# Odd layer of a two-layer decoder step: rotation, turning and convolution beside the input projection, GpSimd's cosine products one chunk behind VectorE's sine products

## The chip, the cores and the metric

The kernel runs on one core of a Trainium2 chip. A core has five engines, each with an instruction stream of its own: TensorE (PE in the rows), VectorE (DVE), ScalarE (ACT), GpSimd (POOL) and SyncE (SP, which here only issues DMAs). They meet only through semaphores and barriers. The metric is device time in microseconds (us) of one launch. Differences of 0.2% (about 4 us) or more can be told from no change.

## What is computed

One inference step of two layers for 528 prompt positions (16 learned ones and 512) and 32 sample positions (8 sequences of 4). The two sets lie side by side as 560 columns all through the kernel. The changed part belongs to layer 1, the odd one:

```
rq, rk, rv, rg, lx, lgate = split(xn @ w_in_odd, 6 parts of 512 columns)
q = rotary(heads(rq), pos);  k = rotary(heads(rk), pos) * 128**-0.5;  v = heads(rv)
rotary(x): concat([x1*cos - x2*sin, x1*sin + x2*cos])        # x1, x2: halves of a head of 128
retention per head and chunk: S_t = gamma*S_{t-1} + k_t^T v_t,  o_t = q_t S_t
hr = silu(rg) * layernorm_per_head(o)
u  = concat([conv_state, lx]);  xc = conv_b + sum_j conv_w[j] * u[:, j:j+T]      # 4 taps
r, ig = sigmoid of two block-diagonal products with xc
hs = linear recurrence (a from r; input from ig, xc and a);  hl = hs * gelu(lgate)
out = concat([hr, hl]) @ w_out_odd
```

RMSNorms stand before and behind it, and a gated feed-forward part follows. Layer 0 has its own mixer and the same kind of feed-forward part.

## The kernel before

**Layout.** Activations are held turned: 128 features on the partitions, 560 positions along the free axis. A "chunk" is one such 128 x 560 block. `proj` (`Pt`, named `projected` in the rows) has room for 28; the odd input projection fills 24: rq 0 to 3, rk 4 to 7, rv 8 to 11, rg 12 to 15, lx 16 to 19, lgate 20 to 23.

**Projection.** Each product is made of three: weights and inputs are split into a high and a low part, and high*high, high*low and low*high are added up. One output chunk is 8 contraction blocks x 3 products x 2 halves of 280 columns, 48 matmuls (L1919). ScalarE makes the high part of a weight piece (`in_high`, L2093), VectorE the low one (`low`, L2272) and copies the finished chunk from PSUM with the row scale (`in_evac`, L2431). There are two weight pieces (`w_h`, `w_l`) and four PSUM tiles of two banks each. SyncE fills a ring of two slots, each with one unit of 256 weight columns (two chunks). The first four chunks are made together with the norm in `first_tiles`; the other twenty in a hardware loop of five turns with four chunks each. All of that lies in `close_layer(0, ...)`, the block that ends layer 0, since the odd projection is joined to the last feed-forward product of layer 0.

**Between the blocks** stands a barrier of all engines. Three blocks follow the projection:

- Rotation. TensorE multiplies each of the eight q and k chunks by a 128 x 128 matrix `swap`, which exchanges the halves with a sign (L2536). VectorE multiplies the result by the sine (L2557), GpSimd the chunk itself by the cosine (L2547), VectorE adds (L2563). ScalarE scales k first (L2526). SyncE loads the rotation table, the retention state (8 DMAs of 256 KB, L2510), the decay table, the convolution state and the gate weights.
- Turning (`transposes`, L486). k and v are brought to position-major order: 12 jobs of 4 transposes; 5 small ones bring the samples' convolution and recurrence state over. VectorE and ScalarE copy the results in turns (L494, L500).
- Retention (`decayed_attention`). TensorE first runs 4 matmuls on constants (`warm`, L465), then 32 score tiles (L981). VectorE multiplies each by its decay (L1084), TensorE multiplies by v (L1004). For the samples' tile of each head it also multiplies by the loaded state (L1014, 8 small products). Behind every second score tile VectorE makes one of 16 steps of the convolution (`convolution`: L2619 and L2620 for the first tap, L2623 and L2625 for the other three).

State update, gates, recurrence, normalisation and layer 1's output projection come behind.

## Time and profile before

| | us |
|---|---|
| three runs, median (lowest, highest) | 1869.51 (1868.13, 1869.68) |
| the profiled run's own time | 1871.89 |
| its span, first to last instruction | 1870.3 |
| TensorE busy | 1683.5 (90% of the span) |
| VectorE / ScalarE / GpSimd busy | 835.4 / 458.2 / 297.3 |
| mean granted TensorE clock, full speed is 1 | 0.928 |

The rows below give times from the start of the span. A timeline row has its start, its length, the engine, the line in the code, the operation and the names written and read; in brackets stands how long the engine was idle before it and what released it. A row of stretches gives each engine's busy time in the stretch with the number of instructions that begin there, then the granted clock (1.00 is 2.4 GHz, 0.50 is 1.2 GHz), the share of the DMA engines and GB/s. Matmuls overlap in the pipeline, so that a matmul of 0.29 us can start every 0.13 us.

### The profile page before, as it was taken

Reading aid. Unit: us, or ns where it says so; the run is one execution under the profiler, and the core shown is the slowest. Engines: PE = TensorE matmul, PEld = TensorE weight load, DVE = VectorE, ACT = ScalarE, POOL = GpSimd, SP = SyncE. Lnnn points to the kernel's source line nnn. Section 1 sums busy time; section 2 is a strip of 40 time slices with the busy share of each in tenths; the row PEclk is TensorE's granted clock in tenths of the full one; section 3 lists DMA queues with packets and bytes.
Section 4 is the critical chain, followed back from the end, with each engine's and each line's share of the span. In section 5 each row is a group of like instructions: output and inputs, shape, how many; then the busy total and the mean of one; then the engine's idle time right before and its main releaser. Section 6 shows DMA issues by size and latency. Waiting matters only on the chain. (4 is left out here: it accounts for less than half of the span.)

```text
span 1870.3 us, 31120 instructions
## 1 busy us (share of the span) xinstructions
PE 1683.5 (90%) x12351; PEld 1539.9 (82%) x12351; DVE 835.4 (45%) x1551; ACT 458.2 (24%) x684; POOL 297.3 (16%) x368
## 2 busy tenths in 40 slices
PE   5999998698876999999999899979579999999996
PEld 4999954465645999999999889957378999999996
DVE  4332544544434664434322463356757544433225
ACT  4111311122212431222212321132334221222211
POOL 1411001001000033333200200030210333332000
PEclk9999987678997999999999899988779999999998
DMA  4322210132975122333333212230131232333321
GB/s 131 94 69 79 68 50 1 51 128 78 285 238 152 46 66 73 86 90 90 93 93 85 68 46 90 88 89 1 51 92 46 68 90 77 80 90 103 83 62 49
DMA packets 225254, 159.80 MB, mean 85 GB/s; under 512 B 18041, under 2 KB 206437, under 8 KB 225048
## 3 DMA queue, kind: packets, MB, share of 16 engines
q1 hardware_dynamic: 220832, 156.40, 28.7%
q0 software_dynamic: 3280, 1.85, 0.4%
q8 instruction: 49, 0.80, 0.2%
q10 hardware_dynamic: 1064, 0.51, 0.1%
q14 instruction: 29, 0.24, 0.0%
HBM read 149.11 MB, written 9.88 MB: 85 GB/s over the span
## 5 line engine op out<-in xcount | busy, mean ns | idle before, releaser
L2093 ACT CAST w_high<-ring 128x1024 fp32r<-128x1024 f32 (+1 forms) x148 | 165.4, 1118 | 749.4 <-PE psum L1919 718.5
L1919 PE MATMUL psum<-mixed_high,w_high 128*128 128x280 f32 x1472 | 310.6, 292 | 20.5 <-DVE mixed_low L2280 18.6
L1919 PE MATMUL psum<-mixed_high,w_low 128*128 128x280 f32 x1472 | 312.2, 293 | 0.0
L1919 PE MATMUL psum<-mixed_low,w_high 128*128 128x280 f32 x1472 | 309.5, 292 | 0.0
L2272 DVE TENSOR_TENSOR w_low<-ring,w_high 128x1024 fp32r<-128x1024 f32 (+1 forms) x148 | 237.3, 1603 | 138.3 <-ACT w_high L2093 136.2
L1919 PEld LDWEIGHTS psum<-mixed_high,w_high 128*128 128x128 f32 x1472 | 235.8, 190 | 21.7 <-DVE w_low L2272 19.4
L1919 PEld LDWEIGHTS psum<-mixed_high,w_low 128*128 128x128 f32 x1472 | 236.3, 190 | 0.0
L1919 PEld LDWEIGHTS psum<-mixed_low,w_high 128*128 128x128 f32 x1472 | 233.8, 189 | 0.0
L2453 POOL TENSOR_TENSOR silu<-silu,rstd 128x560 f32<-128x560 f32 x44 | 61.4, 1394 | 551.7 <-DVE silu L2352 551.7
L2352 DVE TENSOR_TENSOR silu<-silu,psum 128x280 f32<-128x280 f32 x88 | 35.3, 443 | 155.9 <-PE psum L1919 154.3
L348 PE MATMUL psum<-normed_high,w_high 128*128 128x280 f32 x448 | 94.3, 292 | 0.6 <-PEq L531 0.6
L348 PE MATMUL psum<-normed_high,w_low 128*128 128x280 f32 x448 | 93.8, 290 | 0.0
L348 PE MATMUL psum<-normed_low,w_high 128*128 128x280 f32 x448 | 93.5, 290 | 0.0
L1919 PE MATMUL psum<-hidden_low_b,w_high 128*128 128x280 f32 x308 | 90.0, 292 | 0.0
L1919 PE MATMUL psum<-hidden_high_b,w_high 128*128 128x280 f32 x308 | 90.0, 292 | 0.0
L1919 PE MATMUL psum<-hidden_high_a,w_high 128*128 128x280 f32 x308 | 89.8, 292 | 0.0
L1919 PE MATMUL psum<-hidden_high_b,w_low 128*128 128x280 f32 x308 | 89.6, 291 | 0.0
L1919 PE MATMUL psum<-hidden_high_a,w_low 128*128 128x280 f32 x308 | 89.6, 291 | 0.0
L1919 PE MATMUL psum<-hidden_low_a,w_high 128*128 128x280 f32 x308 | 89.5, 291 | 0.0
L1919 PE MATMUL psum<-normed_b,w_high 128*128 128x280 f32 x320 | 88.0, 292 | 0.0
L2352 DVE TENSOR_TENSOR silu<-rstd,psum 128x280 f32<-128x280 f32 x88 | 35.3, 442 | 110.5 <-PE psum L1919 110.3
L348 PEld LDWEIGHTS psum<-normed_high,w_high 128*128 128x128 f32 x448 | 71.1, 188 | 1.1 <-issue 1.1
(460 smaller groups left out, 3289.7 us busy)
## 6 DMA issues: line engine op xcount, KB each, us to landing
ring<-in_ffn_wd SPq DMA_DIRECT2D x16, 1408.0 KB, 7.0
ring<-in_ffn_wg SPq DMA_DIRECT2D x40, 512.0 KB, 4.0
ring<-in_ffn_wu SPq DMA_DIRECT2D x40, 512.0 KB, 5.2
projected<-in_cache_fox_k SPq DMA_DIRECT2D x64, 256.0 KB, 4.3
ring<-in_w_in_even SPq DMA_DIRECT2D x14, 1024.0 KB, 5.3
ring<-in_w_in_odd SPq DMA_DIRECT2D x12, 1024.0 KB, 5.1
v_pages<-in_cache_fox_v SPq DMA_DIRECT2D x32, 256.0 KB, 3.7
projected<-in_cache_fox_v SPq DMA_DIRECT2D x16, 256.0 KB, 3.2
```

What stands on the lines that cost most here:

```text
L348: last = nc.tensor.matmul(banks[2 * tl + half][:, 0:HALF], w[:, k, :], m[:, half * HALF:(half + 1) * HALF], start=(kk == 0 and w is w_high ...
L1919: done = mm(banks[2 * tl + a][:, 0:HALF], w, m[a], start=first and s == 0, stop=last and s == 2)
L2093: nc.scalar.copy(dst, src).then_inc(w_hi[p], 1)
L2272: v.tensor_tensor(dst, src, high_.bitcast(F32), ALU.subtract).then_inc(w_lo[p], 1)
L2352: last = v.tensor_tensor(silu[:, slot, c], silu[:, slot, c] if p else rstd[:, c], banks[2 * q + a][:, 0:HALF], ALU.mult)
L2453: g.tensor_tensor(silu[:, slot, :], silu[:, slot, :], rstd[:, :], ALU.mult)
```

## The change

The rotation block and the turning block go. Their work, and the convolution, is put among the last twenty chunks of the projection, whose loops are written out on every engine:

- The order of the units becomes q, k, lx, v, rg, lgate (`UNITS`). From the ninth chunk on only two PSUM tiles are used in place of four, so that banks 4 to 7 are free for turning.
- Rotation without the matrix: VectorE multiplies each half of a chunk by the sine and writes it to the other half's partitions of a scratch tile (two 64 x 560 products, the sign is in the table). GpSimd multiplies the chunk by the cosine. VectorE adds one chunk later. The scaling of k is four ScalarE instructions.
- The convolution is four VectorE steps, one tap for all four chunks each, behind the chunks n = 14 to 17 in order.
- TensorE turns behind n = 10 and 11 (the small jobs) and behind n = 15 to 20 (two jobs of four transposes each); ScalarE copies all of them.
- Rotation table, convolution state, recurrence state, gate weights and decay tables are loaded during the projection. The retention state is loaded in the retention block, and TensorE waits for it at the first head's samples.
- Memory is laid out anew: the mixer's output lies in `proj`, and the gates' and the recurrence's buffers are tiles of their own. The constant `swap` and its load go.

```diff
             def _(sp):
...
+                    send(sp, units[1], slot, UNITS[slot])
+                    sp.dma_start(decays[slot], io["c_decay"][:, slot, :]).then_inc(decay_in, 16)
...
+                sp.wait_ge(used[1], DOWN_END + 2)
+                sp.dma_start(rope, io["c_rope"]).then_inc(rope_full, 16)
+                sp.dma_start(conv_in, io["state_lru_conv"].rearrange("b j n -> (b j) n")).then_inc(lru_in, 16)
+                sp.dma_start(h0_in[:, :], io["state_lru_h"].rearrange("b (k p) -> (b k) p", p=128)).then_inc(lru_in, 16)
+                for s in range(4, 12):
+                    when_split(29 + s)
+                    send(sp, units[1], s % 2, UNITS[s])
+                    if s == 5:
+                        sp.wait_ge(lru_zero, 1)
...
             def _(pe):
-                with pe.Fori(1, 6) as i:
-                    for q in range(4):
...
+                for n in range(4, 24):
+                    p, t = n % 2, in_tile(n)
+                    pe.wait_ge(w_lo[p], 31 + n // 2)
+                    pe.wait_ge(tile_evac[t], (15, 11, 14, 11)[t] + (1 if n < 8 else 2 + (n - 8) // 2))
...
+                    if n == 15:
+                        pe.wait_ge(rotated, 8)
...
+                    for j in TURNS_AT.get(n, ()):
+                        turn(j)
...
             def _(act):
+                for n in range(4, 24):
+                    if n + 2 < 24:
+                        in_high(n // 4, n % 4)
+                    if 6 <= n < 10:
+                        c = n - 6
+                        act.wait_ge(tile_evac[c], (15, 11, 14, 11)[c] + 2)
+                        nc.scalar.mul(Pt[:, 4 + c, :], Pt[:, 4 + c, :], QK_SCALE).then_inc(rk_scaled, 1)
+                    for j in TURNS_AT.get(n, ()):
+                        act.wait_ge(turned, j + 1)
...
             def _(dve):
+                def rotate(i):
+                    x, tmp = Pt[:, i, :], rtmp[i % 2]
...
+                    v.drain()
+                    v.tensor_tensor(tmp[0:64, :], x[64:128, :], rope[64:128, 1, :], ALU.mult)
+                    v.tensor_tensor(tmp[64:128, :], x[0:64, :], rope[0:64, 1, :], ALU.mult).then_inc(rot_sin, 1)
+                def add_rotated(i):
+                    dve.wait_ge(rot_cos, i + 1)
+                    v.tensor_tensor(Pt[:, i, :], Pt[:, i, :], rtmp[i % 2][:, :], ALU.add).then_inc(rotated, 1)
...
+                for n in range(24):
+                    in_evac(n)
+                    if n == 0:
+                        in_low(0, 1, 33)
+                    if 4 <= n < 22:
+                        in_low((n // 2 + 1) % 2, n % 2, 32 + n // 2)
+                    if 5 <= n < 13:
+                        rotate(n - 5)
+                    if 6 <= n < 14:
+                        add_rotated(n - 6)
...
+                    if 14 <= n < 18:
+                        convolve(n - 14)
             def _(pool):
+                    for i in range(2 * MH):
+                        pool.wait_ge(rot_sin, i + 1)
+                        g.tensor_tensor(Pt[:, i, :], Pt[:, i, :], rope[:, 0, :], ALU.mult).then_inc(rot_cos, 1)
...
 def decayed_attention(...)
+                    if state_in is not None and hd == 0:
+                        pe.wait_ge(state_in, 16 * 8)
```

The names in the rows of the two orders are those of the program; `token_major` holds the products with the sine before the change, `rotated` after it. On TensorE, from the last matmuls of the projection to the first score of the retention, stands before the change:

```order
L1919 MATMUL psum<-normed_b_6575,w_low_6554 128x280
L2079 REGISTER_ALU
L2079 COMPARE_AND_BRANCH
L1860 UNCONDITIONAL_BRANCH
L2528 UNCONDITIONAL_BRANCH
L2536 MATMUL psum<-projected,swap 128x280 x16
L2505 UNCONDITIONAL_BRANCH
L479 UNCONDITIONAL_BRANCH
L486 MATMUL psum<-ident,projected 128x128 x16
L486 MATMUL psum<-ident,projected 16x128 x4
```

The multiplications by `swap` leave the program. The transposes move up to places within the projection. On TensorE behind the chunk n = 15 stands now:

```order
L1961 MATMUL psum<-normed_b_6579,w_high_6557 128x280
L1961 MATMUL psum<-normed_high_a_6577,w_low_6558 128x280
L1961 MATMUL psum<-normed_b_6579,w_low_6558 128x280
L2132 MATMUL psum<-ident,projected 128x128 x8
L1961 MATMUL psum<-normed_high_a_6577,w_high_6557 128x280
L1961 MATMUL psum<-normed_b_6579,w_high_6557 128x280
```

Eight transposes stand there, and the next chunk's 48 matmuls behind them; n = 16 to 20 have the same. On VectorE the rotation block has this piece eight times before the change (two of them shown, behind the block's entry):

```order
L2431 TENSOR_TENSOR projected<-psum,rstd 128x280 x4
L1860 UNCONDITIONAL_BRANCH
L2549 UNCONDITIONAL_BRANCH
L2557 TENSOR_TENSOR token_major<-psum,projected 128x280 x2
L2563 TENSOR_TENSOR projected<-projected,token_major 128x560
L2557 TENSOR_TENSOR token_major<-psum,projected 128x280 x2
L2563 TENSOR_TENSOR projected<-projected,token_major 128x560
```

After the change a chunk's turn on VectorE in the projection (here n = 6 and the start of n = 7) reads:

```order
L2508 TENSOR_TENSOR projected<-psum,rstd 128x280 x2
L2349 TENSOR_TENSOR w_low_6558<-ring,w_high_6557 128x1024
L2519 TENSOR_TENSOR rotated_6549<-projected 64x560
L2520 TENSOR_TENSOR rotated_6549<-projected 64x560
L2525 TENSOR_TENSOR projected<-projected,rotated_6548 128x560
L2508 TENSOR_TENSOR projected<-psum,rstd 128x280 x2
L2349 TENSOR_TENSOR w_low_6558<-ring,w_high_6557 128x1024
```

The copy from PSUM and the low part of the weights keep their place at the head of each turn. The sine products and the sum of the chunk before stand behind them; they were in a block of their own.

## Rows read from the trace of the kernel before

**Rows 1.** Stretches by stage: projection, rotation, turning, retention (columns as above).
```profile
1100.00:1220.00 120.00, 120.00 (x934) 120.00 (x934) 38.37 (x59) 18.89 (x18) 0.00 (x0) 1.00 0.27 88
...
1223.40:1244.10 20.70, 10.28 (x32) 6.73 (x32) 14.60 (x28) 2.06 (x1) 14.57 (x9) 0.77 0.71 197
1244.10:1252.50 8.40, 7.84 (x53) 7.09 (x53) 4.51 (x9) 3.65 (x8) 0.00 (x0) 0.75 0.01 2
...
1256.10:1294.90 38.80, 37.71 (x193) 29.83 (x191) 23.41 (x64) 9.12 (x11) 1.39 (x8) 0.87 0.00 1
```

**Rows 2.** Timeline of TensorE, behind the projection to the first score.
```profile
1223.41 6.64 PE L2536 MATMUL psum<-projected,swap 128*128 128x280 f32 x20 [1.88 <-PEq L128]
...
1244.14 7.42 PE L486 MATMUL psum<-ident,projected 128*128 128x128 f32 x48 [7.58 <-PEq L2505]
1251.48 0.50 PE L486 MATMUL psum<-ident,token_major_v 24*128 24x24 f32 x5
1252.62 3.67 PE L465 MATMUL psum<-ones 128*128 128x512 f32 x8 [0.64 <-PEq L475]
1256.13 0.82 PE L981 MATMUL psum<-projected 128*128 128x256 f32 x4
```

**Rows 3.** Timeline of TensorE in layer 0, the same `warm` and first score.
```profile
243.75 5.86 PE L465 MATMUL psum<-ones 128*128 128x512 f32 x8
249.44 0.82 PE L981 MATMUL psum<-projected 128*128 128x256 f32 x4
```

**Rows 4.** Stretches of 2 us behind the projection's end.
```profile
1224.00:1226.00 2.00, 2.00 (x7) 1.42 (x6) 0.00 (x0) 1.46 (x1) 0.32 (x1) 0.58 0.73 202
1226.00:1228.00 2.00, 2.00 (x6) 1.44 (x5) 0.51 (x2) 0.00 (x0) 0.53 (x1) 0.56 1.05 333
```

**Rows 5.** A stretch of 2 us amid layer 0's transposes.
```profile
228.00:230.00 2.00, 2.00 (x21) 1.91 (x19) 1.49 (x3) 1.32 (x3) 0.00 (x0) 1.00 0.90 258
```

**Rows 6.** Timeline of VectorE in the projection: one chunk and the next one's start.
```profile
1104.27 0.81 DVE L2431 TENSOR_TENSOR projected<-psum,rstd 128x280 f32 x2 [3.37 <-PE psum L1919]
1105.22 1.23 DVE L2272 TENSOR_TENSOR w_low<-ring,w_high 128x1024 fp32r<-128x1024 f32 x1
1110.46 0.81 DVE L2431 TENSOR_TENSOR projected<-psum,rstd 128x280 f32 x2 [4.01 <-PE psum L1919]
```

**Rows 7.** Rotation, by line (ns min/median/max, first and last start): VectorE's sum, GpSimd's product.
```profile
L2563 DVE TENSOR_TENSOR projected<-projected,token_major x8: 744/853/1889, 1228.9 to 1242.7; 128x560 f32<-128x560 f32 x8
```
```profile
L2547 POOL TENSOR_TENSOR projected<-projected x8: 1370/1862/1868, 1227.5 to 1239.3; 128x560 f32<-128x560 f32 x8
```

**Rows 8.** Timeline in a feed-forward stage: GpSimd's product, and VectorE beside it.
```profile
718.80 1.40 POOL L2453 TENSOR_TENSOR silu<-silu,rstd 128x560 f32<-128x560 f32 x1 [7.39 <-DVE silu L2352]
```
```profile
719.00 2.28 DVE L2272 TENSOR_TENSOR w_low<-ring,w_high 128x1024 fp32r<-128x1024 f32 x1 [0.28 <-ACT w_high L2093]
```

**Rows 9.** Groups by line in the retention: busy us, mean ns, idle before.
```profile
L2623 DVE SCALAR_TENSOR_TENSOR convolved<-projected,cols,convolved 128x525 f32<-128x525 f32 (+2 forms) x12 | 9.2, 767 | 1.1
...
L1004 PEld LDWEIGHTS psum<-projected,token_major 128*128 128x128 f32 (+1 forms) x32 | 6.2, 230 | 3.1 <-DVE projected L1084 2.3
...
L2625 DVE SCALAR_TENSOR_TENSOR convolved<-lru_samples,cols,convolved 128x32 f32<-128x32 f32 x12 | 2.9, 246 | 0.0
...
L2619 DVE TENSOR_SCALAR convolved<-projected,cols 128x528 f32<-128x528 f32 x4 | 2.2, 545 | 0.5 <-POOL lru_samples L2608 0.5
```

**Rows 10.** DMAs of the retention state by line, and the first products with it.
```profile
L2510 SPq DMA_DIRECT2D states<-in_state_ret_S x8: 427/630/1339, 1223.8 to 1229.1; - x8
...
DMA to landing us min/median/max: 4.4/5.3/5.9
```
```profile
1263.44 1.95 PE L1014 MATMUL psum<-qs,states 128*128 128x4 f32 x16
```

**Rows 11.** DMA issues of the odd weights: KB each, median us to landing.
```profile
ring<-in_w_in_odd SPq DMA_DIRECT2D x12, 1024.0 KB, 5.1
```

**Rows 12.** A stretch of layer 1's output projection, whose code is written out.
```profile
1380.00:1390.00 10.00, 10.00 (x81) 10.00 (x80) 4.06 (x6) 4.17 (x7) 0.00 (x0) 1.00 0.14 47
```

**Rows 13.** SyncE's queue: issue of the first gate weights.
```profile
1231.67 1.37 SPq L2518 DMA_DIRECT2D projected<-in_lru_wa  x2
```

More of the change, by code:

```diff
@@ L150, in hybrid_decoder @@
     tri_st = sb("tri_st", [128, 128])
-    swap = sb("swap", [128, 128])
     small = sb("small", [128, 84])
@@ L642, in _ @@
         def _(act):
-            for dst, name in ((ones, "ones"), (tri_ts, "tri_ts"), (tri_st, "tri_st"), (swap, "swap"),
+            for dst, name in ((ones, "ones"), (tri_ts, "tri_ts"), (tri_st, "tri_st"),
                               (small, "small"), (smask, "smask")):
@@ L2259, in _ @@
                 normalise(1, (layer + 1, 0), lambda a, k: n_b[:, k, 0] if a else n_h[:, k], lambda a, k: sq_n[k][:, :], in_first)
-                with act.Fori(1, 5) as i:
-                    for q in range(4):
-                        in_high(i, q)
-                for q in range(2):
-                    in_high(5, q)
+                for n in range(4, 24):
[7 more added lines that the diff above has]
+                        act.wait_ge(turned, j + 1)
+                        bank, dst = banks[4 + j % 4], TURNS[j][1]
+                        if j < 4:
+                            src = bank[:, 0:24].rearrange("p (b j) -> p b j", j=3)
+                        else:
+                            src = bank[:, 0:32] if j == 4 else bank[0:dst.shape[0], :]
+                        nc.scalar.copy(dst, src).then_inc(turned_copied, 1)
             @block.vector
@@ L2434, in _ @@
-                for q in range(4):
-                    in_evac(0, q)
-                    if q == 0:
-                        in_low(0, 1, 33)
-                with dve.Fori(1, 5) as i:
-                    for q in range(4):
-                        in_evac(i, q)
-                        in_low(1 - q // 2, q % 2, i * 2 + (32 + q // 2))
-                for q in range(4):
-                    in_evac(5, q)
-                    if q < 2:
-                        in_low(1, q, 42)
+                        last = v.tensor_tensor(Pt[:, at_, HALVES[a]], banks[2 * t + a][:, 0:HALF], rstd[:, HALVES[a]], ALU.mult)
@@ L2484, in hybrid_decoder @@
     left.close()
-    left = ExitStack()
-    xn, inner, states, spare, inner_top, tok = place_mixer()
-    tokf = tok[:, :, :, :].rearrange("p a b c -> p (a b c)")
+    left, inner = ExitStack(), ExitStack()
+    place(left, "below_states", [128, 6160])
+    states, spare, ga_, gt_, hs_ = (place(left, n, shape) for n, shape in (
+        ("states", [128, NB * MH * 128]), ("spare", [128, 6 * FH * VW]), ("input_gate", [128, 4, T]),
+        ("root", [128, 4, T]), ("recurrent", [128, 4, T])))
+    xn = proj[:, 0:KC * T].rearrange("p (k t) -> p k t", k=KC)
@@ L2567, in hybrid_decoder @@
-    jobs = token_major([(TK["mk"], rk), (TK["mv"], rv)])
-    jobs += [([(conv_in[:, c * 128:(c + 1) * 128], 0)],
-              lambda cp_, bank, c=c: cp_(us[:, c, :, 0:3], bank[:, 0:24].rearrange("p (b j) -> p b j", j=3)))
-             for c in range(4)]
-    jobs.append(([(h0_in, 0)], lambda cp_, bank: cp_(h0, bank[:, 0:32])))
-    transposes(jobs)
-    s_us, s_gl, s_gs, s_lm, s_ln2, s_a, s_r = (sem(x) for x in (
-        "new_inputs", "gate_logits", "gates", "lambda_by_scalar", "lambda_by_gpsimd", "decay_done",
+    sparef = spare[:, :]
```

252 lines of the change are left out of this document (122 added, 130 removed).

## The prediction

> **What bounds the kernel now.** I read the stretches by stage first. During the odd projection TensorE begins 934 matmuls in 120 us at full clock, that is 0.1285 us for each, and nothing waits on anything else: VectorE is busy 38.4 us and ScalarE 18.9 us of those 120, GpSimd not at all [rows 1]. In the two blocks behind it that turns round. In the rotation (20.7 us) TensorE's work is 10.3 us, VectorE's 14.6 and GpSimd's 14.6, and the turning is 8.4 us more [rows 1]. So for some 29 us TensorE, which is the bound of the kernel, has little or short work, while for the 120 us ahead three engines stand nearly idle. The timeline gives the edges: the last projection matmul ends at 1223.41 - 1.88 = 1221.53, and the first score begins at 1256.13 [rows 2]. That is 34.6 us, of which the 4 warming matmuls (8 records) take from 1252.62 to 1256.13, 3.5 us. The retention behind it (38.8 us) is TensorE's again, busy 37.7 us of it [rows 1].
>
> **The two blocks go.** After the change the projection's end is followed by one barrier, then the warming, then the first score. The barrier is 1.9 us [rows 2]. The warming costs more than it does now. Behind the projection's end TensorE pauses 1.9 us, and from about 1224 to 1228 the granted clock is 0.58 and 0.56, so mostly 1.2 GHz [rows 4]; now the swap matmuls pay for this under VectorE's cover, later the warming pays. Layer 0 has this case: the same warming took 249.44 - 243.75 = 5.7 us [rows 3]. I take 5.7; 3.5 is the other end. The new distance is 1.9 + 5.7 = 7.6 us in place of 34.6: **-27.0** (-29.2 at the other end).
>
> **The transposes stay, on the path.** TensorE is the bound of the projection, so each transpose put there lengthens it. There are 12 x 4 = 48 of them and 5 small ones, the same as now [rows 2]. Their price now, 7.42 us for 48 [rows 2], contains half clock (0.75 in that stretch) [rows 1]; at full clock 21 begin in 2 us [rows 5], 0.10 us each. So 48 x 0.10 = 4.8, and 0.3 for the five small ones: **+5.1**. The other end is all of them at half clock, twice that, +10.2. The copies don't hold them up: TensorE turns two jobs into two of four free banks behind a chunk, and ScalarE has a whole chunk of 6.19 us to copy them.
>
> The Trainium skill speaks against this edit: the page "TensorE: Matmul & The Clock Gate", Part 4 (PE-mode transpose), says that transposes don't count as work for the clock gate. By that rule the transposes would be no cover, and the clock could fall at the places where they stand. In this trace it doesn't: amid layer 0's transposes the granted clock is 1.00 [rows 5]. The sum goes by the row; the rule's case is a rival below.
>
> **VectorE's additions, hidden.** A chunk takes TensorE 6.19 us (1104.27 to 1110.46 between two copies), of which VectorE works about 2.2 (from 1104.27 to 1105.22 + 1.23) and then idles 4.01 [rows 6]. A rotating turn (eight of them, n = 5 to 13) adds three products or sums over 560 elements: two 64 x 560 sine products, which no row shows, and one sum. A 128 x 560 sum is 0.85 us in the median, 0.74 at least and 1.89 at most [rows 7]. Length along the free axis is what the nearest rows differ by, so I take 0.85 for each, and 2.2 + 3 x 0.85 = 4.7 us is under 6.19. GpSimd's product is 1.40 us alone and 1.86 in the rotation block [rows 7, 8]; it starts when the sine products end, and the sum that needs it stands a whole chunk later, so the wait in front of that sum has 6.19 us for a product of 1.4 to 1.9.
>
> VectorE and GpSimd do get in each other's way. A low part of the weights that takes 1.23 us [rows 6] took 2.28 when GpSimd's product had begun 0.2 us before it, and it ended 1.08 us after that product did [rows 8], as if the one had waited for the other. Per chunk there is one GpSimd product, so at most one such wait of up to 1.86 us: 4.7 + 1.9 = 6.6 us, 0.4 over, for eight chunks 3.3 us in all. Against that VectorE may fall behind by 6.19 - 2.2 = 4.0 us before TensorE misses its weights, since the low part made in turn n is first needed by chunk n + 2. So the cost is 0 either way.
>
> The page "SBUF — State Buffer" of the Trainium skill (Who interferes with whom) has this as a rule: a VectorE instruction with two SBUF inputs and a GpSimd instruction that reads SBUF exclude each other, and the second one blocks until the first ends. The rows just read agree with it.
>
> The convolution adds 4 x (0.77 + 0.25) = 4.1 us to n = 15, 16 and 17, and less to n = 14, where the large steps are 0.55 [rows 9]. 2.2 + 4.1 = 6.3 us; TensorE takes 6.19 + 0.8 = 7.0 for these chunks with their eight transposes. It stays hidden. If the cover were gone, the work moved here is 8 x 2.55 + 14.3 = 35 us of VectorE.
>
> **ScalarE, GpSimd, SyncE.** ScalarE has 18.9 us of work in 120 [rows 1], and it gets four scalings and 17 copies; no turn is near 6.19 us. SyncE issues the rotation table and the two small states ahead of the fifth weight unit, and the four gate weight loads (1.37 us for two of them [rows 13]) ahead of the seventh. A unit lasts 2 x 6.19 = 12.4 us on TensorE and lands in 5.1 [rows 11], so some 7 us are to spare, and the loads queued ahead take less. The two decay tables that ride with the first two units are a quarter of a unit each; they can delay the second one by 5.1 / 4 = 1.3 us at most. I take 0, and leave 1.3 for the upper end. The swap constant's load at the start: 0.
>
> **The state's load.** It starts with the retention block. Before, the eight DMAs begin to be issued at 1223.8 and 1229.1 and land at the latest at 1229.1 + 5.9 = 1235.0, 11.6 us behind their block's start near 1223.4, with the rotation table ahead of them [rows 2, 10]. TensorE comes to the state 1263.44 - 1256.13 = 7.3 us behind the first score [rows 2, 10], so 5.7 + 7.3 = 13 us behind the start. The new wait costs 0. Queued behind it are the state products and all later scores and v products of the retention, and VectorE and ScalarE behind those. Only if the warming takes 3.5 us does TensorE come at 10.8, and could wait 0.8 us.
>
> **The retention without the convolution.** VectorE works 9.2 + 2.9 + 2.2 = 14.3 us and more less there [rows 9]. TensorE's idle time is 38.8 - 37.7 = 1.1 us [rows 1], and its weight loads wait 2.3 us for the decayed scores [rows 9]. Not all of that is the convolution's doing. I take **-1.5**, between -0.5 and -3.4.
>
> **Sum.** -27.0 + 5.1 - 1.5 = -23.4 us. Against the profiled run: 1871.89 - 23.4 = 1848.5. The median is 2.4 us under the profiled run, and my forecast is for the median: 1869.51 - 23.4 = **1846.1**. The known ends: -29.2 + 5.1 - 3.4 = -27.5, 1842.0; and -27.0 + 10.2 - 0.5 + 1.3 = -16.0, 1853.5.
>
> **Rivals.**
> - **VectorE becomes the bound of the rotating chunks.** The one sum of 1.89 us [rows 7] is its row. If all three added instructions took that, a turn would be 2.2 + 5.7 = 7.9 us, 1.7 over, 13.4 for eight; less the 4.0 it may fall behind, +9.4: 1855.5. Against it: seven of eight such sums are near 0.85 with GpSimd at work beside them. It decides from 1.33 us each.
> - **The clock falls at the transposes.** A fall lasts about the stretch 1224 to 1228, at mean clock 0.57, so 4 x 0.43 = 1.7 us are lost [rows 4]. At six places, +10.3: 1856.4. Against it: [rows 5]. This is what the skill's rule on transposes would come to.
> - **Slower than before: TensorE starves for instructions.** The loop's body of four chunks was run five times; now twenty chunks, 960 matmuls and as many weight loads, stand in a row and all must be fetched. The longest wait of TensorE for its own sequencer that doesn't come from another engine's work is the 1.88 us at a block's change [rows 2]. Once per chunk that is 20 x 1.88 = +37.6, net +14.2: 1883.7. It makes the change a loss from 23.4 / 20 = 1.2 us per chunk. Against it: layer 1's output projection is written out too and begins 81 matmuls in 10 us at full clock [rows 12], the loop's pace.
> - **The clock doesn't fall behind the projection.** The warming takes 3.5 us, less up to 0.8 of wait for the state: -1.4 to -2.2, 1844.3. For it nothing but that the pause is short; against it [rows 3, 4].
> - **It doesn't do what it says** (a new wait in the projection, such as the one for `rotated` or for the copied tile, holds TensorE at every chunk). Every such count is reached about a chunk or more ahead by the figures above; 1 us per chunk would give 1866.
>
> **Chances.** Forecast 0.76, no fall behind the projection 0.10, VectorE the bound 0.05, clock at the transposes 0.04, a new wait 0.02, starving 0.03. The range runs from 1 us under the lower end to the case of six clock falls: 1841 to 1856.4; the forecast's own ends lie within it, and what is left out is about 0.1 to 0.15. Faster by over 0.2% (3.7 us, about what a measurement can tell) 0.96, within it 0.01, slower 0.03.
>
> **What would show it.** In the new profile the projection should be about 120 + 5 us long for the same chunks at clock 1.00, with VectorE's idle time behind TensorE still there in every turn, shortest at n = 15 to 17. The warming should be near 5.7 us in a stretch of clock near 0.6, the first score some 7.6 us behind the last projection matmul, no wait for the state at the first head, and the retention 1 to 3 us shorter than 38.8. Wrong would be: idle TensorE between chunks released by VectorE's low part (first rival), a clock under 1.00 between n = 15 and n = 23 (second), TensorE idle with nothing to release it (third).

## The result and the profile after

| | before | after |
|---|---|---|
| median of the runs made side by side, 4 each (lowest, highest), us | 1869.6 (1868.13, 1871.52) | 1851.28 (1844.71, 1854.7) |
| ratio after to before, 95% interval | | 0.9897 (0.9867 to 0.9927) |
| span of the profiled run | 1870.3 | 1853.2 |
| mean granted TensorE clock of the span | 0.928 | 0.925 |

The change makes the kernel 14 to 25 us faster; 23.4 were forecast, and 1851.28 lies in the range. Two later comparisons of the same kernels gave 0.9872 (0.9837 to 0.9906) and 0.9875 (0.9843 to 0.9907). Over all 16 runs of the changed kernel the median is 1848.8, from 1839.84 to 1859.41. Before spreads as widely: its 41 runs in the four comparisons have a median of 1871.07, from 1863.97 to 1885.37, so the two medians are 22.3 us apart. The intervals reach 0.3% to either side, so the 0.2% named at the head is finer than what one such comparison can tell. The profile shown here is that of the slowest of the first four runs.

**The projection.** The stage windows of the changed kernel, with the columns of [rows 1]:

```profile
1106.00:1226.00 120.00, 120.00 (x940) 119.33 (x939) 66.49 (x113) 26.33 (x38) 15.62 (x12) 1.00 0.27 87
```

TensorE is busy throughout at full clock, as in [rows 1]; now 940 matmuls and transposes begin in 120 us. VectorE went from 38.4 to 66.5 us, and GpSimd from nothing to 15.6. The list of who TensorE waited for, over the same chunks n = 4 to 23, has a single line, at n = 4, and before has it too (0.9):

```profile
PE psum L1961 <- DVE projected L2508: 1.0, 1, 1.0
```

**A rotating turn on VectorE**, and GpSimd's product beside it (timelines, one chunk and the next one's start):

```profile
1130.30 0.74 DVE L2519 TENSOR_TENSOR rotated<-projected 64x560 f32<-64x560 f32 x1
1131.05 0.73 DVE L2520 TENSOR_TENSOR rotated<-projected 64x560 f32<-64x560 f32 x1
1131.81 0.74 DVE L2525 TENSOR_TENSOR projected<-projected,rotated 128x560 f32<-128x560 f32 x1
1134.03 0.81 DVE L2508 TENSOR_TENSOR projected<-psum,rstd 128x280 f32<-128x280 f32 x2 [1.47 <-PE psum L1961]
1135.11 1.23 DVE L2349 TENSOR_TENSOR w_low<-ring,w_high 128x1024 fp32r<-128x1024 f32 x1 [0.28 <-ACT w_high L2160]
```
```profile
1131.86 1.95 POOL L2589 TENSOR_TENSOR projected<-projected 128x560 f32<-128x560 f32 x1 [4.28 <-DVE rotated L2520]
```

Against [rows 6] the idle time behind TensorE shrank from 4.01 to 1.47 us and did not vanish. A product with the sine is 0.74 us, and so is the sum. The convolution's turns are hidden too: behind n = 15 to 17 VectorE still waits 1.18 or 1.19 us for TensorE, and behind n = 14, whose turn on TensorE has no transposes, 0.95 us.

**Behind the projection** stands what [rows 2] had in three blocks:

```profile
1226.31 0.29 PE L1961 MATMUL psum<-normed_b,w_low 128*128 128x280 f32 x1
1228.55 3.67 PE L460 MATMUL psum<-ones 128*128 128x512 f32 x8 [1.95 <-PEq L124]
1232.06 0.82 PE L976 MATMUL psum<-projected 128*128 128x256 f32 x4
...
1238.95 0.40 PE L999 MATMUL psum<-spare,token_major 32*128 32x32 f32 x2
1239.28 2.03 PE L1011 MATMUL psum<-qs,states 128*128 128x4 f32 x14
```

The first score comes 5.75 us behind the last projection matmul's start. (The prediction counts from that matmul's end, 0.29 us later.) No wait stands before the first product with the state, 7.2 us behind the first score, as in [rows 2, 10].

**Where the time went, by phase.** The starts of TensorE's instructions cut each profile into phases. "To score" runs from the start of the last projection matmul to that of the first score, "retention" from there to the first gate product, "update" from there to the first sum of the head norm. The profiles of the experiments are added here, so that one table serves for all:

| us | fifth chunk starts | projection | to score | retention | update | span |
|---|---|---|---|---|---|---|
| before | 1097.7 | 123.56 | 34.89 | 39.75 | 29.75 | 1870.3 |
| e9_before_again | 1096.5 | 123.57 | 34.96 | 39.46 | 38.04 | 1877.2 |
| after | 1096.7 | 129.62 | 5.75 | 38.44 | 37.74 | 1853.2 |
| e1_again | 1093.4 | 129.64 | 7.45 | 36.78 | 31.32 | 1840.4 |
| e8_after_third | 1093.2 | 129.69 | 7.45 | 36.88 | 29.66 | 1842.1 |
| e2_no_warm | 1092.9 | 129.63 | 2.25 | 40.82 | 30.90 | 1839.3 |
| e3_fill | 1095.9 | 129.67 | 7.45 | 36.87 | 31.61 | 1846.0 |
| e4_conv_back | 1098.1 | 129.68 | 7.45 | 39.06 | 32.20 | 1850.5 |
| e5_turns_twice | 1094.0 | 135.21 | 5.75 | 38.33 | 30.88 | 1849.9 |
| e6_same_turn | 1099.0 | 129.67 | 7.45 | 36.87 | 29.65 | 1847.9 |
| e7_sines_thrice | 1094.0 | 137.79 | 7.43 | 38.46 | 37.82 | 1860.3 |
| e10_state_by_head | 1096.8 | 129.65 | 2.24 | 38.51 | 38.05 | 1849.7 |
| e11_and_one_seam | 1098.1 | 129.58 | 2.25 | 38.36 | 31.33 | 1843.8 |

The projection is the same to 0.1 us wherever its code is the same. With the warming and without the convolution "to score" and "retention" each come in two sizes, but their sum is 44.1 to 44.4 in after, e1, e3, e5, e6 and e8 (45.9 in e7), against 74.6 and 74.4 before: -30.3. The update is 30 to 32 us, or 38. What lies before the fifth chunk, and is the same code but for a constant that is no longer loaded, varies by 6 us. Between the two profiles first compared: -1.0 before the fifth chunk, +6.1, -30.4, +8.0, and +0.3 for the rest, together -17.1.

### The profile page after: what moved, and what is told of

The parts are those of the page before. It is cut to its first block and busy times, and to the rows that moved or that the text cites. A ratio compares the mean times of both kernels' runs of the same rounds, so it can differ in the third digit from the quotient of the medians.

```text
span 1853.2 us, 30899 instructions
## 1 busy us (share of the span) xinstructions
PE 1681.5 (91%) x12319; PEld 1537.5 (83%) x12319; DVE 833.2 (45%) x1542; ACT 460.8 (25%) x696; POOL 298.0 (16%) x368
```

## The experiments

Theory: two blocks in which TensorE had little to do went, their transposes cost TensorE its stream's time and nothing more, and everything else is covered; what the runs differ by beyond that is TensorE's clock. Rivals: VectorE's or GpSimd's cover is accidental or absent, the transposes cost by the places and not by their number, and the long fallen clock in the update belongs to the new layout.

### Where the clock falls: the same kernels again

`e1_again` and `e8_after_third` are the changed kernel, `e9_before_again` is the kernel before.

> The changed kernel once more, unchanged. In its first profile everything up to the end of the retention was 25.4 us shorter than before, and the state update behind it 8.0 us longer (37.7 in place of 29.8 us from the first gate product to the first sum of the head normalisation), in a stretch whose granted clock was 0.50. Theory A, the clock falls in the state update in some executions and not in others: the times spread between some 1844.5 (1869.6 - 5.07 of a longer projection way, sign turned: +5.1 - 29.1 - 1.3 + 0.2) and 1853, and each profile's state update is either near 29.8 us or longer by several us at clock 0.50. Theory B, the new layout or order makes the state update longer always: every profile shows some 37.7 us there, and the spread of the times has another place.

> The changed kernel once more, for the chip of this job and for one more profile of where the clock falls. Theory A (the long stretch of half clock in the state update, and the clock at full speed or not in the warming, differ from execution to execution): one or both places look different from the first profile of the changed kernel: distance from the last projection matmul to the first score 5.7 or 7.5 us, state update 30 to 38 us, and the time follows the mean clock of the run, between 1840 and 1855. Theory B (they belong to the layout): the same 5.7 and 37.7 us as in the first profile.

> The kernel before once more, for a second profile of where its clock falls. Theory A (the falls in the retention and behind it come in every kernel of this case and differ by execution in place and length): the distance of 34.9 us between the last projection matmul and the first score stays within 1.5 us, the state update lies between 29.6 and 38 us, and the granted clock falls to 0.50 four or five times in the retention here too. Theory B (the long falls belong to the changed layout alone): the state update is 29.8 us again; a value above 33 here would refute B.

Measured: 1842.98 (1839.84 to 1859.41, 6 runs) and 1848.79 (1843.62 to 1855.34, 6 runs), and for before 1878.88 in its one run. A fall is in what follows a stretch at the granted clock 0.50 (1.2 GHz) with 1.00 before and behind it. The update's rows show the clock behind the times. This is one stretch each, the same instructions, of before, of before again and of after:

```profile
1295.90:1325.60 29.70, 22.95 (x88) 14.30 (x89) 26.91 (x116) 14.98 (x26) 5.54 (x4) 0.90 0.00 1
```
```profile
1294.50:1332.60 38.10, 31.31 (x89) 18.55 (x89) 25.66 (x116) 15.09 (x27) 5.59 (x4) 0.64 0.00 1
```
```profile
1270.50:1308.20 37.70, 30.99 (x88) 18.49 (x88) 25.73 (x116) 14.99 (x26) 5.50 (x4) 0.65 0.00 1
```

88 or 89 matmuls take 30 us at a mean clock of 0.90 or 38 us at 0.64 or 0.65, and both kernels show both. So the +8.0 in the update isn't the change's. By one profile of each kernel it would have looked like its price.

What goes with the long update is where the falls lie against the program. These are the first 2 us behind the first gate product, of before and of before again:

```profile
1295.88:1297.88 2.00, 2.00 (x5) 1.49 (x6) 1.91 (x14) 1.25 (x1) 0.00 (x0) 0.53 0.04 12
```
```profile
1294.53:1296.53 2.00, 2.00 (x6) 1.52 (x7) 1.91 (x14) 1.53 (x2) 0.00 (x0) 0.64 0.04 12
```

A fall begins about 0.1 us behind the first gate product in the one and about 0.5 us behind it in the other. In the four profiles with an update near 38 us, the mean clock of this row is 0.64, 0.64, 0.68 and 0.69. In the other nine it is 0.50 to 0.59 (six), 0.75 (`e4_conv_back`) or 1.00 (`e2_no_warm`, `e5_turns_twice`). So a few tenths of a microsecond in the place of a fall go with 8 us later on. This is read from 13 profiles; no run sets that place on purpose.

The same holds, in small, behind the projection. In `e1_again` the warming runs into a fallen clock, as [rows 4] have it:

```profile
1225.31 5.37 PE L460 MATMUL psum<-ones 128*128 128x512 f32 x8 [1.96 <-PEq L124]
1230.51 0.81 PE L976 MATMUL psum<-projected 128*128 128x256 f32 x4
```
```profile
1225.00:1227.00 2.00, 1.69 (x4) 0.99 (x5) 0.00 (x0) 1.65 (x3) 0.00 (x0) 0.92 0.18 48
1227.00:1229.00 2.00, 2.00 (x3) 0.67 (x2) 0.00 (x0) 1.95 (x4) 0.68 (x3) 0.50 1.06 307
1229.00:1231.00 2.00, 2.00 (x6) 0.98 (x5) 0.00 (x0) 1.99 (x2) 0.66 (x3) 0.73 1.04 290
```

In after the warming ran at 1.00, but the clock fell later, in the retention:

```profile
1240.00:1242.00 2.00, 2.00 (x14) 2.00 (x14) 0.00 (x0) 0.22 (x1) 0.00 (x0) 0.64 0.01 4
1242.00:1244.00 2.00, 2.00 (x7) 1.59 (x7) 0.29 (x1) 0.19 (x1) 0.00 (x0) 0.50 0.00 0
1244.00:1246.00 2.00, 2.00 (x7) 1.65 (x6) 0.88 (x2) 0.37 (x1) 0.00 (x0) 0.50 0.00 0
```

The retentions as wholes, after first, `e1_again` second:

```profile
1232.00:1270.70 38.70, 37.65 (x194) 30.09 (x193) 10.85 (x33) 9.79 (x13) 0.75 (x4) 0.87 0.15 39
```
```profile
1230.51:1267.29 36.78, 35.73 (x193) 28.38 (x192) 10.66 (x32) 7.85 (x12) 0.00 (x0) 0.91 0.11 27
```

What the warming gained (1.7 us) the retention paid (1.7). The kernel before has this pattern in its retention too, about every 10 us:

```profile
1265.00:1267.00 2.00, 2.00 (x9) 1.80 (x9) 0.87 (x2) 0.41 (x1) 0.00 (x0) 0.57 0.00 0
1275.00:1277.00 2.00, 2.00 (x10) 1.82 (x10) 0.82 (x2) 0.41 (x1) 0.00 (x0) 0.63 0.00 0
1285.00:1287.00 2.00, 2.00 (x11) 1.82 (x12) 0.80 (x2) 0.41 (x1) 0.00 (x0) 0.69 0.00 0
```

Read in stretches of 2 us, one such fall takes 1.7 us of full clock away. Before has three of them from the first score to the first gate product, and what is the length of four more between the projection's end and the first score. After and `e1_again` have the length of three from the projection's end to the first gate product, wherever they lie.

### No warming

```diff
-                warm(3)
+                if state_in is None:
+                    warm(3)
```

> The changed kernel without the 4 warming matmuls ahead of the retention. They took 3.5 us at full clock in the profile of the changed kernel (1228.55 to 1232.06). If they do nothing for the clock behind the projection: -3.5 us, less a wait for the retention state of up to 2.6 us (the last load was issued at 1232.9 and landed up to 5.4 us later, 1238.3; the state would be wanted at 1239.28 - 3.5 = 1235.8): -0.9 to -3.5. If they keep the clock up: the scores run at 0.5 for some 3.4 us, +1.7, so -1.8 to +0.8. The first product with the state would start at about 1235.8 or, waiting, up to 1238.3.

Measured: 1847.63 (1840.83 to 1850.2), ratio 0.9875 (0.9856 to 0.9894), no different from the changed kernel. To the first gate product 43.1 us in place of 44.2. The warming's 5.2 us are gone, and 4.0 of them come back in the retention, of which 0.8 are a wait for the state:

```profile
1233.34 0.40 PE L1000 MATMUL psum<-spare,token_major 32*128 32x32 f32 x2
1234.53 1.96 PE L1012 MATMUL psum<-qs,states 128*128 128x4 f32 x16 [0.79 <-DMA states<-in_state_ret_S]
```

The rest is the clock: the mean over this retention is 0.83, with the first scores under it.

```profile
1224.82:1265.64 40.82, 38.99 (x192) 31.24 (x193) 10.65 (x32) 12.92 (x18) 1.34 (x6) 0.83 0.19 52
```

### Filling the update's idle places

```diff
+        for _ in range(2 if i >= 6 else 1):
             for half in range(2):
...
         if at == 2:
+            warm(6, 1)
             pe.wait_ge(s_gs, 6)
```

The last two gates' products are made twice and one warming matmul is added, some 2.1 us of work.

> The changed kernel with a little useless TensorE work in the state update: one matmul on constants (0.9 us) where TensorE waits 0.97 us for ScalarE ahead of the second head, and the products of the last two gates made twice (1.2 us). Theory A with idle time of TensorE as the cause of the fall: the state update stays at full clock, near 29.8 + 1.2 = 31 us in the profile, and the times gather at some 1846 with little spread. Theory A with another cause of the fall: as e1_again, 0 to 1.2 us longer, with the same spread. Theory B: some 38 to 39 us in the state update.

Measured: 1846.03 (1843.41 to 1848.2, 5 runs), ratio 0.9862 (0.984 to 0.9884); update 31.61 us at mean clock 0.88.

```profile
1269.90:1301.50 31.60, 25.68 (x99) 16.21 (x99) 25.76 (x116) 15.00 (x27) 5.55 (x4) 0.88 0.00 1
```

Inconclusive. None of its five runs is above 1848.2, where 9 of the changed kernel's 16 are; but its median is only 2.8 us under theirs, and its one profile shows an update like `e1_again`'s. Nor does that profile test the filling: the mean clock of its first 2 us behind the first gate product is 0.50, and no unfilled profile with 0.50 to 0.59 there has the long fall either.

### The convolution back in the retention

The four `convolve` steps leave the projection, and one step stands behind every second score tile again, as in [rows 9].

```diff
-                    if 14 <= n < 18:
-                        convolve(n - 14)
...
-                      lambda_by_scalar, lambda_by_gpsimd, None, load_ret_state, s_st2)
+                      lambda_by_scalar, lambda_by_gpsimd, convolution, load_ret_state, s_st2)
```

> The changed kernel with the convolution back in the retention, behind every second score tile, and no longer beside the projection. My term for it was 1.5 us (0.5 to 3.4); the two profiles give 37.05 - 35.74 = 1.3 us from the first score to the last head's state products. Expected: that distance is 37.0 us again, the projection is as long as in the changed kernel (VectorE then idles 3.9 us instead of 0.95 to 1.2 us in n = 14 to 17), and the total is 1.3 us longer, if the clock in the state update doesn't cover it up. The rival, that the convolution costs TensorE something beside the projection: the projection is shorter by over 0.3 us.

Measured: 1848.91 (1846.95 to 1852.11), ratio 0.9879 (0.986 to 0.9899). The projection is unchanged, the retention 39.06 in place of 36.8 to 36.9 in `e1_again`, `e3_fill`, `e6_same_turn` and `e8_after_third`, which have the same distance to the score: **2.2 us** more. The stretch as a whole:

```profile
1235.30:1274.30 39.00, 37.57 (x193) 29.59 (x192) 23.40 (x64) 7.79 (x12) 0.00 (x0) 0.87 0.11 27
```

TensorE is busy 37.6 us in place of 35.7 with the same 193 matmuls, at 0.87 in place of 0.91, and its idle time is 1.4 us in place of 1.05. So 1.8 of the 2.2 us is one more fall of the clock, and 0.4 TensorE standing idle, waiting for VectorE's decayed scores (0.7 us in place of 0.3). The fall needn't be the convolution's: `e7_sines_thrice`, without it, has as many falls up to the first gate product as this run, and its retention is 38.46, only 0.6 us under 39.06. Before and after have equally many in the retention and differ by 1.3 us (39.75 and 38.44). So with equal falls the convolution costs some 0.6 to 1.3 us there.

### The transposes twice

```diff
-                    if j < 5:
+                    for _ in range(2) if j < 5 else ():
...
-                    else:
+                    for _ in range(2) if j >= 5 else ():
```

> Every transpose in the projection is made twice: 53 more. Price theory (a transpose costs its place in TensorE's stream and nothing else): the stretch from the projection's fifth chunk to its last matmul is 129.6 us in four profiles of the changed kernel; it grows by the large jobs' 48 x 0.106 = 5.1 us, and by little for the small jobs, whose 0.46 us per place is a fixed cost of the seam and not of the transpose: 134.7 to 135.2, at granted clock 1.00. Copies by ScalarE stay hidden. Seam theory (most of the 6.1 us is the change of work between matmuls and transposes at eight places, not the transposes): it grows by less than 3 us, under 132.6. Clock theory (transposes are no cover for the clock once there are 1.7 us of them in a row): the granted clock falls below 1.00 behind n = 15 to 20, and the stretch grows by 10 us or more.

Measured: 1851.51 (1851.46 to 1854.05, 4 runs), ratio 0.989 (0.9852 to 0.9928); projection 135.21, +5.55 us for 53 more transposes, at clock 1.00. This stretch holds the six places of n = 15 to 20, with 16 transposes in a row at each:

```profile
1169.70:1217.20 47.50, 47.50 (x386) 46.97 (x385) 22.52 (x43) 12.68 (x19) 0.00 (x0) 1.00 0.24 79
```

The copies on VectorE mark the chunks. A chunk with eight large transposes takes 7.04 us against 6.18 without, and 7.91 with sixteen: 0.86 and 0.87 for each eight, **0.108 us a transpose**, and nothing for the place. For the small ones it is otherwise: three cost 0.47 us, six 0.67; two cost 0.42, four 0.59. So 0.07 to 0.09 each, and some **0.25 per place**. In all 48 x 0.108 + 0.9 = 6.1, which is what the projection grew by. The price theory stands; the seam theory holds for the small ones alone.

### The sum in the same turn

```diff
-                    if 6 <= n < 14:
-                        add_rotated(n - 6)
+                    if 5 <= n < 13:
+                        add_rotated(n - 5)
```

> GpSimd's cosine product is no longer one chunk behind: VectorE adds in the same turn in which it made the sine products, and waits for GpSimd there. Cover theory: the turn on VectorE is then 0.81 + 1.23 + two sine products and a drain, about 1.6, + GpSimd's product 1.4 to 1.9 + the sum 0.74 = 5.8 to 6.3 us, against TensorE's 6.19, and it may fall behind by 4.0: the projection keeps its 129.6 us, and the whole time is that of the changed kernel within 2 us. The lag of one chunk buys nothing here. Rival (the lag is needed: the wait for GpSimd with its semaphores costs more than the products' lengths): turns of 6.8 us or more, eight of them 0.6 over = 5 us less 4.0, so the projection gets 1 us or more longer, and TensorE has idle time released by VectorE's low part of the weights.

Measured: projection 129.67, no change; 1850.1 (1843.98 to 1859.64), ratio 0.9885 (0.9849 to 0.9921). VectorE's turn and GpSimd's product:

```profile
1130.18 0.81 DVE L2508 TENSOR_TENSOR projected<-psum,rstd 128x280 f32<-128x280 f32 x2
1131.32 1.22 DVE L2349 TENSOR_TENSOR w_low<-ring,w_high 128x1024 fp32r<-128x1024 f32 x1 [0.33 <-ACT w_high L2160]
1132.63 0.74 DVE L2519 TENSOR_TENSOR rotated<-projected 64x560 f32<-64x560 f32 x1
1133.38 0.73 DVE L2520 TENSOR_TENSOR rotated<-projected 64x560 f32<-64x560 f32 x1
1135.63 0.74 DVE L2525 TENSOR_TENSOR projected<-projected,rotated 128x560 f32<-128x560 f32 x1 [1.51 <-POOL projected L2589]
1136.37 0.81 DVE L2508 TENSOR_TENSOR projected<-psum,rstd 128x280 f32<-128x280 f32 x2
```
```profile
1134.20 1.39 POOL L2589 TENSOR_TENSOR projected<-projected 128x560 f32<-128x560 f32 x1 [4.83 <-DVE rotated L2520]
```

The 1.47 us of idle time behind TensorE have become 1.51 behind GpSimd, and a turn is 1136.37 - 1130.18 = 6.19 us, TensorE's own pace. The lag of one chunk, half of what the change is named for, buys no time here. It buys room: without it VectorE's turn has no idle time left but a wait for GpSimd.

### The sine products three times

```diff
-                    v.tensor_tensor(tmp[0:64, :], x[64:128, :], rope[64:128, 1, :], ALU.mult)
-                    v.tensor_tensor(tmp[64:128, :], x[0:64, :], rope[0:64, 1, :], ALU.mult).then_inc(rot_sin, 1)
+                    for rep in range(3):
+                        if rep:
+                            v.drain()
+                        v.tensor_tensor(tmp[0:64, :], x[64:128, :], rope[64:128, 1, :], ALU.mult)
+                        last = v.tensor_tensor(tmp[64:128, :], x[0:64, :], rope[0:64, 1, :], ALU.mult)
+                    last.then_inc(rot_sin, 1)
```

> VectorE makes the two sine products three times over in each of the eight rotating turns (the same values). Cover theory of the prediction: a rotating turn has about 4.6 us of work and 1.5 idle; 2 x (2 x 0.737 + a drain of 0.1) = 3.1 us more makes it 7.7 against TensorE's 6.19, 1.5 over; eight times that is 12, less the 4.0 by which VectorE may fall behind before TensorE misses its weights: the projection grows by about 8 us (6 to 9), from 129.6 to about 138, and TensorE shows idle time released by VectorE's low part from about the third or fourth rotating turn on. Rival (VectorE isn't bound by the lengths of its instructions, its idle time is larger than shown): growth under 3 us. Other rival (no slack of 4 us, TensorE waits at once): growth of 12 us or more, with idle time from the first rotating turn on.

Measured: projection 137.79, **+8.1 us**; 1859.26 (1846.65 to 1863.32, 8 runs), ratio 0.9915 (0.9886 to 0.9945). TensorE's waits in it:

```profile
PE psum L1961 <- DVE w_low L2349: 6.9, 6, 1.4
PE psum L1961 <- DVE projected L2508: 1.0, 1, 1.0
```

The arithmetic of the cover (the turn's sum against 6.19 us, less 4.0 of lead) gave 8 us. That it came so close is in part luck. The eight turns took 61.9 us together, 12.4 over TensorE's pace, where 12 were expected, and TensorE's own turns behind n = 10 and 11 are 0.9 us longer for the small transposes, which the sum left out: 12.4 - 0.9 - 4.0 = 7.5, against 8.1. The six waits make 6.9 of these 8.1; the other 1.2 stand in no wait of the profile. The first wait comes at n = 10, in the chunk whose low part VectorE makes in the fourth rotating turn, as expected. So the cover is real, it is 1.5 us per turn, and the rival "VectorE becomes the bound" is what happens once it is used up. The turns also show the two engines in each other's way, GpSimd's product and VectorE's next instructions:

```profile
1136.68 1.94 POOL L2593 TENSOR_TENSOR projected<-projected 128x560 f32<-128x560 f32 x1 [5.86 <-DVE rotated L2523]
```
```profile
1136.63 0.74 DVE L2529 TENSOR_TENSOR projected<-projected,rotated 128x560 f32<-128x560 f32 x1
1137.29 0.80 DVE L2508 TENSOR_TENSOR projected<-psum,rstd 128x280 f32<-128x280 f32 x2
1138.00 1.70 DVE L2349 TENSOR_TENSOR w_low<-ring,w_high 128x1024 fp32r<-128x1024 f32 x1
```

### The state by head, and the small transposes moved

`e10_state_by_head` has no warming and loads the state in four parts, each with a semaphore of its own:

```diff
+        by_head = Cst.rearrange("p (b h) v -> p b h v", h=MH)
+        for hd in range(MH):
+            sp.dma_start(by_head[:, :, hd, :], io["state_ret_S"][:, hd].rearrange("b k v -> k b v")).then_inc(s_st2[hd], 16)
...
-                    if state_in is not None and hd == 0:
-                        pe.wait_ge(state_in, 16 * 8)
+                    if state_in is not None:
+                        pe.wait_ge(state_in[hd], 16)
```

> No warming matmuls, and the retention state is loaded by head in four DMAs, TensorE waiting for each head's own part in place of all eight DMAs at the first. Theory (without warming, the wait for the state is what is late): without warming the first product with the state came 9.7 us behind the first score, with warming 7.2, so 2.5 us were wait; a head's part should land about 5 us after the queue's start, 7.2 us behind the last projection matmul, and be needed at 2.25 + 7.2 = 9.5: no wait. From the last projection matmul to the first gate product 43.1 us become 40.6 to 41, against 44.2 with warming, and the whole 1.2 + 2.3 = 3.5 us shorter than the changed kernel. Rival 1 (the warming pays for the clock, whose falls move into the retention without it): the products wait no longer, but the retention is longer by as much, 43 to 44 us in all. Rival 2 (a load by head, with 512 byte pieces 2 KB apart, is slower): the first head's part lands after 9.5 and the wait is there again, 43 us or more.

`e11_and_one_seam` adds `TURNS_AT = {10: range(0, 4), 15: range(4, 7), ...}`.

> As the run before, and the five small transposes are moved: four behind n = 10, the fifth with the large jobs behind n = 15, none behind n = 11. Seam theory (each place where TensorE goes from chunks to transposes and back costs about 0.4 us beside its transposes): the stretch from the fifth chunk to the last projection matmul falls from 129.67 to 129.2 or 129.3. Rival (each small transpose costs 0.15 to 0.2 us wherever it stands): it stays at 129.6 to 129.7.

Measured: 1840.8 (1837.85 to 1852.18), ratio 0.9833 (0.9797 to 0.987), and 1844.9 (1840.05 to 1849.71), ratio 0.9847 (0.9815 to 0.988). From the start of the last projection matmul to the first gate product 40.75 and 40.61 us, against 44.1 to 44.4: **3.5 us** less. All of these profiles have the length of three falls on that way, so the 3.5 us are what the four warming matmuls cost at full clock (3.5 in after). The wait is gone:

```profile
1237.21 0.40 PE L1000 MATMUL psum<-spare,token_major 32*128 32x32 f32 x2
1237.54 1.95 PE L1012 MATMUL psum<-qs,states 128*128 128x4 f32 x16
```

The sum came as expected, its parts did not. I had taken 2.5 us for the wait, but the row of `e2_no_warm` says 0.8. The other 1.5 are clock: this retention has a mean of 0.87 where that one had 0.83, one fall less. Whether the missing wait did that, or the draw, two profiles of `e10` and `e11` against one of `e2` don't settle. The medians point the same way (12 runs of the two have a median of 1843.8, 16 of the changed kernel 1848.8), but the intervals of the ratios overlap.

The moved small transposes gained 0.07 us, where 0.4 was expected. Four at n = 10 cost 0.54 us, and the fifth made the place at n = 15 cost 1.17 in place of 0.86, so 0.31 by itself. The 0.25 goes with a group of small transposes, also where it stands directly ahead of large ones, and not with leaving the chunks. What it is stays open; 0.15 of it stands in the profile as issue ahead of the group's weight loads, that is as waiting for nothing that it shows.

## Why the prediction was right, point by point

- **The two blocks' end: right, for a partly wrong reason.** From the last projection matmul's end, 7.6 us to the first score were forecast with the fallen clock and 5.4 without. Of eight profiles with warming, six gave 7.14 or 7.16 and two 5.46 (0.29 more in the table). The 0.4 us too much is the warming, 5.7 forecast and 5.2 measured: in layer 0 the clock is 0.50 from before the warming's start to over 4 us into it, which [rows 3] don't show, while here it falls only about 1 us into it. The choice between the two, which I argued from layer 0 [rows 3, 4], didn't matter: in the two profiles without a fall in the warming it came in the retention, and the two phases together are 44.1 to 44.4 us either way (45.9 in `e7_sines_thrice`, whose clock fell in both). The rival "the clock doesn't fall" showed its sign in the profile and brought nothing in time.
- **Retention: the right sign, the size only in part the convolution's.** -1.5 was forecast for the convolution, from idle times [rows 1, 9], with no term for the clock. The retention is 1.3 us shorter than before where it has as many falls (after), and 2.9 to 3.0 where it has one less. `e4_conv_back` gives -2.2 with one fall less, `e7_sines_thrice` against it -0.6 with as many. Whether the convolution brings a fall about stays open. With the clock's share, both terms together were -28.5 by the forecast and -30.3 measured.
- **Transposes: +5.1 forecast, +6.1 measured.** The large ones were right (48 x 0.10 by [rows 5], 48 x 0.108 measured). The undersized term is the five small ones, 0.3 for 0.9. I had scaled them by their number from a row of their own block [rows 2] and left out what it costs to put them between other work.
- **The clock at the transposes (rival): refuted.** The granted clock is 1.00 in every stretch of the projection, and stays there with sixteen transposes, 1.7 us, in a row in `e5_turns_twice`. Under a row of transposes alone the clock is even seen to rise. In layer 0 of the kernel before, 96 fp32 transposes follow each other for 12 us (224.69 to 236.8), behind 3.7 us of idle time. Their start runs at 0.50, and TensorE does nothing else when the clock rises:

```profile
226.00:228.00 2.00, 2.00 (x12) 1.97 (x12) 0.98 (x2) 0.59 (x1) 0.00 (x0) 0.59 0.92 269
...
234.00:236.00 2.00, 2.00 (x21) 1.94 (x20) 1.62 (x3) 1.21 (x3) 0.00 (x0) 1.00 0.00 0
```

  On this the Trainium skill's page "TensorE: Matmul & The Clock Gate", Part 4 (PE-mode transpose), would have had it otherwise; its measurement is for bf16, and these rows of fp32 transposes don't agree with it.
- **VectorE hidden: right**, 1.5 us of idle time left per rotating turn (4.7 of 6.19 forecast). `e7_sines_thrice` shows that the sum and the lead of 4.0 us were the right way to compute it, to about 0.6 us. The least idle time wasn't at n = 15 to 17, as forecast, but at n = 14 (0.95 us): its turn is 0.9 us shorter on TensorE, and the convolution's steps behind n = 15 to 17 took 3.5 us in place of 4.1.
- **GpSimd beside VectorE: right in cost, wrong in who pays.** I let VectorE wait for GpSimd. In the changed order VectorE's sum begins 0.05 us before GpSimd's product, and it is the product that takes 1.95 us in place of 1.40; the sum keeps its 0.74. That it is the later one that waits is what the Trainium skill says on the page "SBUF — State Buffer" (Who interferes with whom), and these rows agree.
- **A new wait, starving, loads: none.** The rival on the other side, 1.88 us per chunk for instructions, was worth nothing: the written-out loop keeps 0.128 us per matmul.
- **What wasn't in the sum:** the clock in the update, 0 or +8 us, and 6 us before the fifth chunk. Both are the same in kind for either kernel and are not the change's, but the range had to hold them. It did so with the places meant for other rivals.
- The net by phases: +6.1 - 30.3 = -24.2, forecast -23.4. The two misses, +1.0 and -1.8, go against each other, and that is luck.

## What to carry to other kernels

When a stage is bound by one engine and the next leaves it idle, merge them by the turn: sum each engine's instructions per turn, compare with the bound engine's turn, and allow for the lead it may lose once. Here that sum held when it was put to the test (8 us expected, 8.1 measured, 7.5 by the turns as they came out). What must run on the bound engine costs its stream time (0.108 us a transpose), and small groups put between other work cost some 0.25 us each on top.

Before a difference in a stage that the change doesn't touch is explained, profile both kernels again. Here 8 us of difference turned up in the old kernel, too.

## What the runs showed of the hardware

- **A clock fall that is avoided in one place may be paid in the next.** Full clock in the warming (5.75 for 7.45 us) was followed both times by a retention longer by as much (38.4 for 36.8). Warming is worth nothing here: without it, and with the state in time, the way to the first gate product is 3.5 us shorter, with falls of the same length in all.
- **A long fall.** In 4 of 13 profiles, of both kernels, TensorE stays at a granted clock of 0.50 from some 14 us behind the first gate product to the update's end, some 24 us; two rows of it from after:

```profile
1288.00:1298.00 10.00, 9.03 (x22) 5.48 (x22) 3.73 (x23) 7.24 (x12) 1.37 (x1) 0.50 0.00 0
1298.00:1308.00 10.00, 5.43 (x13) 2.58 (x11) 5.67 (x20) 1.24 (x2) 0.00 (x0) 0.50 0.00 0
```

  In the other nine the same update takes 29.7 to 32.2 us, at a mean clock of 0.78 to 0.90 where I read it. It came where the fall at the first gate product began some 0.5 to 0.8 us behind it, and in none of the nine other profiles. What sets that place wasn't found.
- **VectorE and GpSimd in turns, both ways.** GpSimd's 128x560 product: 1.39 us with VectorE idle, 1.95 when VectorE's sum began 0.05 us before. VectorE's low part: 1.23 us alone, 1.70 in `e7_sines_thrice` when GpSimd's product was under way at its start; it ended 1.08 us after that product did, like the pair in [rows 8].
